# Two blocks in fp32: gates by tanh, a third score bank, spectra products in two parts, and a written order of cross attention

## What is computed

```
def attention_mixer(q, k, v, qn, kn, cos, sin):      # 8 heads of 64, 2 of keys and values
    ...
        s = jnp.einsum("bkgqd,bktd->bkgqt", qblk, k).astype(F32) * scale
        p = jax.nn.softmax(s, axis=-1).astype(v.dtype)
        return jnp.einsum("bkgqt,bktd->bkgqd", p, v)

def long_conv(u, spec, skip):
    L = u.shape[1]
    uf = u.astype(F32)
    y = jnp.fft.irfft(jnp.fft.rfft(uf, n=2 * L, axis=1) * spec, n=2 * L, axis=1)[:, :L]
    return (y + uf * skip.astype(F32)).astype(u.dtype)

def hyena_mixer(u, conv_w, spec, skip):
    u = short_conv(u, conv_w)
    v, x1, x2 = jnp.split(u, 3, axis=-1)
    z = x1 * long_conv(v, spec[:, 0], skip[0])
    return x2 * long_conv(z, spec[:, 1], skip[1])
```

## Time and profile before

| | us |
|---|---|
| median of 3 runs (lowest, highest) | 3742.75 (3738.45, 3746.29) |
| the profiled execution | 3736.58 |
| its span on the core | 3734.6 |
| PE busy | 3489.3 |
| mean granted clock of PE | 0.957 |

### The profile page before, as it was taken

One profiled execution on the slowest core, in us unless ns is written; L12 is line 12 of the kernel. 1 busy time (PEld: TensorE's weight loads), 2 busy tenths in 40 slices (PEclk: granted clock), 3 DMA queues, 4 the chain that ended last, 5 costly groups with the idle time before them and its releaser, 6 DMA issues.

```text
span 3734.6 us, 40819 instructions
## 1 busy us (share of the span) xinstructions
PE 3489.3 (93%) x15452; PEld 2741.1 (73%) x15452; DVE 1691.3 (45%) x2613; ACT 1466.8 (39%) x2149; POOL 1742.9 (47%) x1336
## 2 busy tenths in 40 slices
PE   8999999999999978999898999998789998989999
PEld 6777787777787766667786788877665777768887
DVE  5466434376536784445433321267654445333120
ACT  3344633334644334544344322233354434443221
POOL 4453344453345673234362555557622434526564
PEclk9999999999999988998899999999898989999999
DMA  4322234222224322121251433332311214414332
GB/s 154 100 79 79 71 110 147 82 89 72 82 93 142 107 85 86 62 62 55 95 178 57 131 108 96 121 107 79 112 63 46 70 53 141 138 65 145 101 96 90
DMA packets 128843, 359.50 MB, mean 96 GB/s; under 512 B 16767, under 2 KB 17087, under 8 KB 128649
## 3 DMA queue, kind: packets, MB, share of 16 engines
q1 hardware_dynamic: 128648, 356.91, 29.6%
HBM read 322.24 MB, written 25.17 MB: 93 GB/s over the span
## 4 chain that ended last, share of the span: by engine, by line
PE 76%; DVE 13%; issue 3%; ACT 3%; POOL 2%; DMA 1%; SPq 1%; DVEq 0%; ACTq 0%; POOLq 0%
PE B L813 22%; PE B L815 22%; PE B L814 22%; PE B L940 1%; PE B L857 1%; PE B L962 1%; PE B L1064 1%; POOL WSP L1464 1%; PE B L1119 1%; PE B L1101 1%; DVE B L1564 1%; DVE RXA L1783 1%; SPq L2168 1%; DVE RXA L1581 1%; POOL FACC L1514 1%
## 5 line engine op out<-in xcount | busy, mean ns | idle before, releaser
L1464 POOL TENSOR_TENSOR WSP<-WRAW,WSP 128x512 fp32r<-128x512 f32 x1088 | 1432.9, 1338 | 1760.5 <-ACT WSP L1134 1760.2
L813 PE MATMUL B<-H,WSP 128*128 128x512 f32 x2496 | 1023.9, 410 | 100.2 <-POOL WSP L1464 68.5
L814 PE MATMUL B<-H,WSP 128*128 128x512 f32 x2496 | 991.5, 397 | 0.0
L815 PE MATMUL B<-H,WSP 128*128 128x512 f32 x2496 | 991.1, 397 | 0.0
L1134 ACT ACTIVATE WSP<-WRAW 128x1024 fp32r<-128x1024 f32 (+1 forms) x600 | 583.5, 976 | 691.9 <-PE B L815 528.5
L813 PEld LDWEIGHTS B<-H,WSP 128*128 128x128 f32 x2496 | 482.1, 193 | 253.7 <-POOL WSP L1464 60.9
L814 PEld LDWEIGHTS B<-H,WSP 128*128 128x128 f32 x2496 | 482.3, 193 | 105.0 <-issue 7.8
L815 PEld LDWEIGHTS B<-H,WSP 128*128 128x128 f32 x2496 | 480.4, 192 | 104.9
L1564 DVE TENSOR_TENSOR B<-B,RN 128x512 f32<-128x512 f32 x194 | 135.1, 696 | 491.5 <-PE B L815 491.3
L813 PE MATMUL B<-YM,WSP 128*128 128x512 f32 x512 | 199.4, 390 | 0.0
L815 PE MATMUL B<-YM,WSP 128*128 128x512 f32 x512 | 199.2, 389 | 0.0
(11 more groups left out here) (422 smaller groups left out, 5521.5 us busy)
## 6 DMA issues: line engine op xcount, KB each, us to landing
WRAW<-in_wb SPq DMA_DIRECT2D x318, 512.0 KB, 3.6
WRAW<-in_wa SPq DMA_DIRECT2D x154, 512.0 KB, 3.7
WRAW<-in_wa SPq DMA_DIRECT2D x48, 256.0 KB, 2.6
WRAW<-in_wb SPq DMA_DIRECT2D x48, 256.0 KB, 2.7
WRAW<-in_wd SPq DMA_DIRECT2D x16, 512.0 KB, 3.9
QA<-RXA SPq DMA_DIRECT2D x64, 64.0 KB, 2.0
PA<-xs SPq DMA_DIRECT2D x16, 256.0 KB, 3.0
xs<-PA SPq DMA_DIRECT2D x16, 256.0 KB, 4.3
```

The source lines that it names most:

```text
L813: e.matmul(o, L[0], R[0], start=first, stop=False)
L814: e.matmul(o, L[0], R[1], start=False, stop=False)
L815: return e.matmul(o, L[1], R[0], start=False, stop=last)
L1464: x = e.tensor_tensor(WSP[:, i % NSP, 1, c:c + CUT], WRAW[:, i % NRAW, c:c + CUT], WSP[:, i % NSP, 0, c:c + CUT].bitcast(fp32), ALU.subtract)
```

## The change

1. Every sigmoid of a gate becomes tanh(x/2), a function of the exponential's table. Since sigmoid(x) = (tanh(x/2) + 1)/2, `by` multiplies by (t + 1) in one instruction, and the half is put into the split of M.
2. Attention b has a third bank for scores (O, in turn with S0 and S1), and the last branch of the second block too; its split of M comes one unit later.
3. `uim` has two parts of three products each; `needs` lets a `park` or another filling stand between them.
4. With new costs in `needs`, the order of attention b changes: for `by` of odd number in a pair 0 to 2, the turn and normalising of a block come first.
5. WL lies in a tile of its own, is zeroed and loaded at the unit `vs` (values of attention b).
6. `cross` has its order written out.

The core of the diff:

```
@@ -146,13 +146,13 @@
     if k == "sc":
         ab, l, c, i = a
         n = [(("qrope", ab, l, c), 3.4), (("krope", ab, l, c if ab == "a" else 0), 7.4 if ab == "a" else 9.0)]
-        n.append((("sc", ab, l, c, i - 1) if i else ("sc", ab, l, c - 1, 3), 2.2 if ab == "a" else 4.4))
+        n.append((("sc", ab, l, c, i - 1) if i else ("sc", ab, l, c - 1, 3), 2.2 if ab == "a" else 3.0))
         return n + ([(("sel", l, i, 16), 1.0)] if ab == "a" and i else [])
     if k == "nrm":
         return [(("sc", *a), 4.4 if a[0] == "a" else 4.0)]
     if k == "tr":
         ab, l, c, i = a
-        return [(("nrm", *a), 2.0), (("tr", ab, l, c, i - 1) if i else ("tr", ab, l, c - 1, 3), 1.2)]
+        return [(("nrm", *a), 2.0 if ab == "a" else 1.0), (("tr", ab, l, c, i - 1) if i else ("tr", ab, l, c - 1, 3), 1.2)]
     if k == "pv":
         return [(("tr", *a, 3), 1.4), (("atty", *a[1:2], a[2] - 1) if a[0] == "a" else ("bsplit", a[1], a[2] - 1), 1.6)]
     if k == "atty":
...
@@ -232,9 +232,12 @@
         l, o, j2 = a
         return [(("usplit", l, o, 3), 2.5)] + ([] if o else [(("fspec", l, 1, 1), 5.0)])
     if k == "ysplit":
-        return [(("uspec", *a), 9.0)]
+        return [(("uim", *a, 1), 4.5)]
     if k == "uim":
-        return [(("uspec", *a), 0.0)]
+        l, o, j2, part = a
+        return [(("uspec", l, o, j2), 4.0), (("uim", l, o, j2, 0) if part else ("uim", l, o, 0, 1), 4.5)][:1 + part + j2]
+    if k == "park":
+        return [(("uspec", a[0], int(a[1] >= 5), 1), 0.0)]
     if k == "hxr":
         return [(("tokx", *a, 3), 1.5), (("fsum", *a, 0), 6.0)]
     if k == "inv":
...
@@ -410,7 +413,8 @@
         tokens += [Unit("tokx", l, i, t=i < 3, pj=i == 3) for i in range(4)] + [Unit("hxr", l)]
         for o in range(2):
             for j2 in range(2):
-                tokens += [Unit("uspec", l, o, j2, w=[("dft", "f", j2, l, o)]), Unit("uim", l, o, j2)]
+                tokens.append(Unit("uspec", l, o, j2, w=[("dft", "f", j2, l, o)]))
+            tokens += [Unit("uim", l, o, j2, part) for j2 in range(2) for part in range(2)]
             tokens += [Unit("ysplit", l, o, 0), Unit("ysplit", l, o, 1)]
             for j in range(4):
                 tokens.append(proj("inv", l, o, j, src=("Y", (l, o, j // 2)), w=[("dft", "i", j, l, o)]))
...
@@ -466,8 +470,9 @@
         last = [Unit("gld", l)]
         for c in range(8):
             last.append(proj("by", "b", l, 2, c, False, True, src=("YC", B), w=[(*B, "br", 2, c)]))
-            last.append(Unit("split", "M", B, c))
-        last += out_product(x, "wo", l, "b", ("M", B))
+            if c:
+                last.append(Unit("split", "M", B, c - 1))
+        last += [Unit("split", "M", B, 7)] + out_product(x, "wo", l, "b", ("M", B))
         return out + merged(memory(l), last)
 
     def memory(l):
...
@@ -489,15 +494,21 @@
             return [proj("xq", l, hd, kk, src=H, w=[(*B, "xq", 2 * hd + kk)]) for kk in range(2)] + [
                 Unit("xqss", l, hd, pj=True)]
 
-        q = xq(0)
-        out = after_norm(x, q[0])
-        side = q[1:] + [u for hd in range(1, 4) for u in xq(hd)]
-        scores, values = [], []
-        for hd in range(4):
-            scores += [Unit("xsc", l, hd, s=True), Unit("xnrm", l, hd), Unit("xtr", l, hd, t=True)]
+        def turned(hd):
+            return [Unit("xnrm", l, hd), Unit("xtr", l, hd, t=True)]
+
+        def values(hd):
+            out = []
             for dc in range(2):
-                values += [Unit("xpv", l, hd, dc, pj=True), Unit("split", "YX", l, 2 * hd + dc)]
-        return out + merged(scores, values, side) + out_product(x, "xo", l, "b", ("YX", l))
+                out += [Unit("xpv", l, hd, dc, pj=True), Unit("split", "YX", l, 2 * hd + dc)]
+            return out
+
+        q = [xq(hd) for hd in range(4)]
+        sc = [Unit("xsc", l, hd, s=True) for hd in range(4)]
+        out = after_norm(x, q[0][0]) + [q[0][1], q[1][0], q[0][2], sc[0], q[1][1], q[2][0], q[1][2]] + turned(0) + [sc[1], q[2][1]]
+        out += values(0) + [q[2][2], sc[2]] + turned(1) + q[3][:2] + turned(2) + [q[3][2], sc[3]]
+        out += values(1) + values(2) + turned(3) + values(3)
+        return out + out_product(x, "xo", l, "b", ("YX", l))
 
     def mlp(l, aux):
         x = 4 + 3 * l
...
@@ -782,6 +793,14 @@
 
             return (dve_done, ("wlo", i)) if rest_by_dve[i] else (lo_done, i)
 
+        def merge_bank(ab, c):
+
+            return (S0, S1)[c % 2] if ab == "a" else (S0, S1, O)[c % 3]
+
+        def score_bank(ab, i, hh):
+
+            return (S0, S1)[hh] if ab == "a" else (S0, S1, O)[(2 * i + hh) % 3]
+
         def index_bank(c, i, hh):
             return ((S0, S1), (T1, O))[(3 * c + i - 1) % 2][hh]
 
...
+            def sigmoid(u, o, *tag):
+
+                w.wait_ge(dve_done, ("scaled", u.pj))
+                e.activation(o, pj(u)[:, :], ACT.Tanh, scale=0.5).then_inc(*act_done.up(("pj", u.pj), *tag))
...
@@ -1520,21 +1545,24 @@
                         w.wait_ge(act_done, ("tokx", l, j))
                         e.tensor_tensor(HX[:, j, :], HX[:, j, :], FACC[:, 0, :], ALU.mult).then_inc(*pool_done.up((k, l, j)))
                 elif k == "uim":
-                    l, o, j2 = a
+                    l, o, j2, part = a
+                    s = (l, o, j2)
                     U, F = spectrum("uspec", o, j2), spectrum("fspec", o, j2)
                     t3, t4 = terms(j2)[2:]
-                    w.wait_ge(pool_done, ("facc", l, 1, 3, 1))
-                    w.wait_ge(dve_done, ("half", 1, "uspec", *a))
-                    e.tensor_tensor(t3, U[1], F[1], ALU.mult).then_inc(*pool_done.up(("m0", *a)))
-                    w.wait_ge(dve_done, ("half", 3, "uspec", *a))
-                    e.tensor_tensor(t4, U[3], F[3], ALU.mult).then_inc(*pool_done.up(("m1", *a)))
-                    w.wait_ge(pool_done, ("m1", *a))
-                    e.tensor_tensor(t3, t3, t4, ALU.subtract).then_inc(*pool_done.up(("re1", *a)))
-                    w.wait_ge(pool_done, ("re1", *a))
-                    e.tensor_tensor(F[1], U[3], F[1], ALU.mult).then_inc(*pool_done.up(("m2", *a)))
-                    e.tensor_tensor(F[3], U[1], F[3], ALU.mult).then_inc(*pool_done.up(("m3", *a)))
-                    w.wait_ge(pool_done, ("m3", *a))
-                    e.tensor_tensor(F[3], F[3], F[1], ALU.add).then_inc(*pool_done.up(("im1", *a)))
+                    if part == 0:
+                        w.wait_ge(pool_done, ("im1", l, o, 0) if j2 else ("facc", l, 1, 3, 1))
+                        w.wait_ge(dve_done, ("half", 1, "uspec", *s))
+                        e.tensor_tensor(t3, U[1], F[1], ALU.mult).then_inc(*pool_done.up(("m0", *s)))
+                        w.wait_ge(dve_done, ("half", 3, "uspec", *s))
+                        e.tensor_tensor(t4, U[3], F[3], ALU.mult).then_inc(*pool_done.up(("m1", *s)))
+                        w.wait_ge(pool_done, ("m1", *s))
+                        e.tensor_tensor(t3, t3, t4, ALU.subtract).then_inc(*pool_done.up(("re1", *s)))
+                    else:
+                        w.wait_ge(pool_done, ("re1", *s))
+                        e.tensor_tensor(F[1], U[3], F[1], ALU.mult).then_inc(*pool_done.up(("m2", *s)))
+                        e.tensor_tensor(F[3], U[1], F[3], ALU.mult).then_inc(*pool_done.up(("m3", *s)))
+                        w.wait_ge(pool_done, ("m3", *s))
+                        e.tensor_tensor(F[3], F[3], F[1], ALU.add).then_inc(*pool_done.up(("im1", *s)))
                 elif k == "ginside":
                     l, hp, hh = a
                     for d in range(2):
...
@@ -1727,6 +1758,9 @@
                         w.wait_ge(dve_done, rope_before("a", l, "iq", c, 2))
                     by_factor(u, rope_tiles("a", "iq", c)[0]).then_inc(*dve_done.up(("pj", u.pj), ("x", "a", l, "iq", c)))
                 elif k == "vs":
+                    l = a[0]
+                    w.wait_ge(dve_done, ("half", 0, "fspec", l, 1, 1))
+                    e.memset(WL[0:32, 0, :], 0.0).then_inc(*dve_done.up(("wlz", l)))
                     by_factor(u, VF[:, 0, :]).then_inc(*dve_done.up(("pj", u.pj), (k, *a)))
                 elif k == "ikw":
                     w.wait_ge(mm_done, (k, *a))
...
@@ -1850,11 +1884,11 @@
                         w.wait_ge(act_done, ("gate", ab, l, br, c))
                     w.wait_ge(mm_done, (k, *a))
                     if first:
-                        e.tensor_tensor(part, pj(u)[:, :], sg, ALU.mult).then_inc(
+                        e.scalar_tensor_tensor(part, sg, 1.0, pj(u)[:, :], ALU.add, ALU.mult).then_inc(
                             *dve_done.up(("pj", u.pj), ("by", ab, l, br, c)))
                         continue
-                    b = banks[(S0, S1)[c % 2]][:, :] if last else pj(u)[:, :]
-                    e.tensor_tensor(b, b, sg, ALU.mult).then_inc(*dve_done.up(("by0", ab, l, br, c)))
+                    b = banks[merge_bank(ab, c)][:, :] if last else pj(u)[:, :]
```

(16 more changed lines are left out.)

24 lines of the change are left out of this document (12 added, 12 removed).

## The result

The changed kernel takes **3698.64 us** (median of 4 runs, 3697.85 to 3700.52), the kernel before 3743.07 in the same comparison. The ratio is 0.9883 with a 95% interval of 0.9866 to 0.9900. That is 44 us less at the medians, where I had forecast 26. The profiled executions, 3736.58 and 3699.23, differ by 37.3: 6 to 7 of the 44 are the distance of the profiled execution of before from its median, which I had carried over as if it belonged to both. The time lies inside the stated range, but between two of its rivals: under the 3704 to 3731 of my own forecast A and over the 3689 of B.

A forecast was written before the change was run, and what follows sets the result against it. PE, busy 93% of 3734.6 us, bounds the kernel, so only its idle stretches and the slow clock behind them pay. Terms −6 −10 −6 −7 +0 +3 = −26 take 3742.75 to 3717; range 3688 to 3741.

The forecast's parts named there:

- forecast A: Whole kernel: the prediction's own case, the summed gain of 26 us, giving 3704 to 3731; chance 0.50.
- B: Rival for the spectra: every rest lands in time, inv 0 waits only for ysplit 0; 28 more, 3689; chance 0.14.
- Spectra (−6): Second block's spectra: POOL's rests come between products, about 3 us less per layer; inv 0 at T+48.5, T being first uspec's start.
- Attention, pairs 0 to 2 (−10): Attention b, six passages: the wait moves, half clock behind it is 3.40 us instead of 6.80; 10 us less (0 to 20).
- Pair 3 (−6): Attention b, pair 3: table loads gone and next scores earlier, so the product with V starts earlier; 3 us less per layer.
- Tables elsewhere (0): Other table loads: 55 fewer on ACT, hidden behind waits for DVE's scaling; 0, up to 4 us less.
- WL (−7): WL's earlier load: the wait of 3.17 becomes about 1.3 for DVE's LR, without the slow clock; 7 us less.
- Last branch (0): Last branch: `by` waits for the same split of M by position on DVE's queue; 0, to 4 us less.
- Cross (+3): Cross attention: waits of 13.9 against 14.1, slower clock 7.0 against 5.5; 1.4 us more per layer, 3 in all.
- Rival E: Behind each of 26 new gaps half clock lasts 6.80 us, not 3.40; 18 us slower in all, 3761; chance 0.08.

The follow-up runs named there:

- u_spec: The changed kernel with the order of the spectra put back as before: 3710.82 us, ratio 0.9917 to the kernel before.
- u_last: The changed kernel with the last branch in two banks and the split of M right behind its unit again: 3696.91 us, ratio 0.9881 to the kernel before.
- u_cross: The changed kernel with the order of cross attention as `merged` makes it again: 3694.27 us, ratio 0.9873 to the kernel before.
- d_lr: The changed kernel with two more memsets of RST ahead of DVE's scaling of LR, lengthening the GLA front's wait: 3711.10 us, ratio 0.9919 to before.
- best1: The changed kernel with `vs` and `k` exchanged, K's exchange behind the loads, and cross in the earlier order with waits filled: 3673.97 us, ratio 0.9823 to before.

## Why the prediction was right, and where its terms were off

The sign and the range are right; the sum of 26 was 11 short of the 37 that the profiled executions differ by, and the median added the 6 to 7 above. The rank of the parts is right only in that attention comes first: undone, it is worth 31, the tables 14, the spectra and WL 12 each, where the forecast had 16, 0, 6 and 7. That the sum is as near as it is, is partly luck. The spectra gave 3.3 of 6; the last branch gave 2.5 where nothing was forecast; and GLA gave 10.9, of which the sum had only 3.4, the clock behind WL's wait.

**Spectra (−6).** The schedule was close where it was worked out: park 3 waits 3.5 (3.8 forecast), park 4 waits 1.2 (1.4 to 3.1), inv 0 starts at T+46.0 (48.5). What I left out lies behind that point: the four inv of o=0 take 2.4 and 3.3 longer than before, and between inv 0 and inv 3 of o=1 10 us of the 12 to 13 won come back, as a wait for the second half's HY on DVE and one behind SP's queue. The stages gained 3.3 in these two traces, 7 against u_spec.

**Attention, pairs 0 to 2 (−10).** What happens is what was forecast: the wait moves with its size kept (2.12 to 2.01) and the half clock of 6.80 becomes 3.40, or none in the third passage of each layer, which I hadn't foreseen. The stretch up to the gate ahead of pair 3 is 6.2 shorter in layer 0 and 7.2 in layer 1, 13 in all, with 0.2 more idle time and 9.6 and 10.8 us less half clock. Why the half clock is shorter (my reason was the work behind the wait) isn't shown.

**Pair 3 (−6).** The product with V starts 2.7 and 3.0 earlier against the gate ahead of it: 5.7. The size is right, the reason only half: 0.9 and 1.3 of it are less waiting in the chain, the rest is clock, with 2.7 and 2.9 us less at half clock.

**Tables elsewhere (0).** Alone they give nothing in attention and 3.8 in all, and no wait in GLA became shorter by them. That they are hidden was right; that hidden means worthless was the failed step: with the other parts in place their removal is worth 14, and 9.9 of it is the length of the two GLA stages, as clock. How a load that PE doesn't wait for comes to change PE's clock isn't shown.

**WL (−7).** The wait fell by 1.8 and 1.5, and the 3.4 us of half clock behind it are gone in both layers, as forecast. Undoing it costs 12, because of GLA again.

**Last branch (0).** u_last differs by 0.0002 in the ratio; its two stages are 0.6 and 1.4 longer, inside the stated 0 to −4.

**Cross (+3).** u_cross is 4 faster, and the reason is the one given: about the same waiting with more half clock. The waits of my schedule, 13.9 in seven pieces, came out as 13.2: 0.7, 3.7, 2.2, 2.1, 0.8, 2.8 and 0.8. Against the old order's longer length of 102.6 the cost is nothing, so +3 is right for one of its two lengths.

**Rival E** (behind each new gap the clock is down for longer) was wrong in attention and right for five of the eight gaps in cross. The step missing from the whole sum is one that no term had: a change of a wait goes with another half clock in the stages behind it. The 10.9 of GLA are such clock. d_lr shows the coupling, most cleanly in layer 1; which of the earlier waits puts GLA into its short form, and whether there is a still shorter one, is open.

## What to carry to other kernels

Where PE is busy over 90%, compare its busy time as well as its waits: with an unchanged count of matmuls, a fall is clock. Count the half clock with the waits: in cross 13.2 us of waiting with four pieces of 2 to 4 took as long as 14.2 with one of 6, or 1.7 longer, so splitting a long wait won nothing here, and filling waits (best1: 7.4 left) did. Undo each part in the final kernel and also try it alone: here the parts undone sum to 67 us by their ratios while the whole is 44 (and the bank is worth 31 undone and 13 alone), so the values of the parts don't add up. When the last link of a wait is a fast engine, follow it back to the queue that issued the load.
